# Attention scores on one Trainium2 core: three paired 64-row passes against two stacked 128-row passes a head

## The reference, cut to what matters

```
# first block, "fox": causal attention with a forget term
logits = einsum('bhtd,bhsd->bhts', qb, kb) * d**-0.5 + F[t] - F[s]
probs  = softmax(where(mask, logits, -inf)); o = probs @ v
y_f    = o * silu(fg)

# second block, layer B, "nb": neighbourhood attention on a 64-wide grid plus 256 context tokens
s      = einsum(q_r, k_reg) * scale + bias;  s_ctx = einsum(q_r, kc) * scale
p      = softmax(concat([s, s_ctx]));        o = p_lat @ v + p_ctx @ vc
y      = (o * silu(g)) @ w_out
```

## Time and profile before

| | |
|---|---|
| median of the runs | 3241.89 us |
| span of the profiled execution | 3236.3 us (first to last instruction; the timed runs are 5.6 us longer in the median) |
| PE busy | 3109.7 us, 96% |
| PEld busy | 2578.9 us, 80% |
| DVE busy | 1999.7 us, 62% |
| ACT busy | 1299.9 us, 40% |
| POOL busy | 759.8 us, 23% |
| fox turns | from 603 to 1210 us |
| nb turns | from 2347 to 3110 us |

### The profile page before, as it was taken

How to read it: one execution, slowest core, us unless ns; L and a number is a source line. 1 busy time by engine, 2 the same in 40 slices (tenths; PEclk the granted TensorE clock), 3 DMA queues, 4 the chain that set the end, 5 groups by cost and what they waited for, 6 DMA issues and landing times.

```text
span 3236.3 us, 47842 instructions
## 1 busy us (share of the span) xinstructions
PE 3109.7 (96%) x18134; PEld 2578.9 (80%) x18134; DVE 1999.7 (62%) x3834; ACT 1299.9 (40%) x2340; POOL 759.8 (23%) x324
## 2 busy tenths in 40 slices
PE   9999999999999989999899999999899999999987
PEld 6888888777777767877799889888677778777765
DVE  5676677555565657975755555556755555655555
ACT  5534443444444440022444444440344444454412
POOL 3223332322222213543211121113112112111221
PEclk9999999999999999999999999999999999999999
DMA  3111111111111137521200010153201111100141
GB/s 118 46 40 46 46 59 46 60 59 53 53 53 53 64 146 298 220 79 52 91 30 30 31 43 30 46 203 130 78 21 51 45 51 45 51 32 33 67 161 76
DMA packets 64828, 237.79 MB, mean 73 GB/s; under 512 B 7008, under 2 KB 10080, under 8 KB 63600
## 3 DMA queue, kind: packets, MB, share of 16 engines
q1 hardware_dynamic: 31680, 115.91, 9.9%
q10 hardware_dynamic: 32944, 119.10, 9.7%
HBM read 185.11 MB, written 49.87 MB: 73 GB/s over the span
## 4 chain that ended last, share of the span: by engine, by line
PE 79%; DVE 9%; ACT 5%; issue 2%; DVEq 2%; DMA 1%; ACTq 1%; SPq 0%
PE ps L1304 21%; PE ps L189 13%; PE ps L360 9%; PE ps L2223 7%; PE ps L1368 5%; PE ps L1334 4%; PE ps L1350 4%; PE ps L891 3%; PE ps L482 3%; PE ps L868 2%; PE ps L133 2%; DVE fox_l L1455 1%; PE ps L852 1%; DVE wa_l L941 1%; PE ps L853 1%
## 5 line engine op out<-in xcount | busy, mean ns | idle before, releaser
L210 POOL TENSOR_TENSOR w_hi<-raw,small 128x1024 fp32r<-128x1024 f32 x160 | 334.9, 2093 | 2393.7 <-PE ps L1304 1099.3
L212 POOL TENSOR_TENSOR w_lo<-raw,w_hi 128x1024 fp32r<-128x1024 f32 x160 | 424.8, 2655 | 22.8
L1304 PE MATMUL ps<-nb_u_hi,w_hi 128*128 128x512 f32 (+1 forms) x640 | 249.2, 389 | 6.1 <-DVE nb_q_lo L2470 4.2
L1304 PE MATMUL ps<-nb_u_hi,w_lo 128*128 128x512 f32 (+1 forms) x640 | 246.6, 385 | 0.0
L1304 PE MATMUL ps<-nb_u_lo,w_hi 128*128 128x512 f32 (+1 forms) x640 | 245.7, 384 | 0.0
L1466 DVE TENSOR_TENSOR nb_pt_lo<-ps,nb_pt_hi 128x512 fp32r<-128x512 f32 x208 | 143.9, 692 | 144.2 <-ACT nb_pt_hi L1393 143.9
L360 PE MATMUL ps<-u_hi,w_hi 128*128 128x512 f32 x528 | 212.8, 403 | 5.9 <-ACT silu_h L539 2.6
L1304 PE MATMUL ps<-u_hi,w_lo 128*128 128x512 f32 x512 | 208.9, 408 | 0.0
L360 PE MATMUL ps<-u_hi,w_lo 128*128 128x512 f32 x528 | 208.6, 395 | 0.0
L360 PE MATMUL ps<-u_lo,w_hi 128*128 128x512 f32 x528 | 208.4, 395 | 0.0
L1304 PE MATMUL ps<-u_hi,w_hi 128*128 128x512 f32 x512 | 208.3, 407 | 0.0
(11 more groups left out here) (357 smaller groups left out, 8027.8 us busy)
## 6 DMA issues: line engine op xcount, KB each, us to landing
raw<-in_w_stream SPq DMA_DIRECT2D x160, 512.0 KB, 3.3
h_sb<-in_w_ada ACTq DMA_DIRECT2D x16, 1024.0 KB, 5.0
nf_b<-nf_rows ACTq DMA_DIRECT2D x16, 512.0 KB, 4.4
nb_bias<-in_rel_bias ACTq DMA_DIRECT2D x16, 448.0 KB, 3.8
y_parts<-wa_y_hi ACTq DMA_DIRECT2D x8, 640.0 KB, 3.0
y_parts<-wa_y_lo ACTq DMA_DIRECT2D x8, 640.0 KB, 4.2
la_out_yh<-y_parts SPq DMA_DIRECT2D x8, 640.0 KB, 10.0
la_out_yl<-y_parts SPq DMA_DIRECT2D x8, 640.0 KB, 11.1
```

The costliest lines, as they stand in the source:

```text
L210: pool.tensor_tensor(w_hi[:, s, :], raw[:, s, :], zero, ALU.add)
L212: pool.tensor_tensor(w_lo[:, s, :], raw[:, s, :], w_hi[:, s, :].bitcast(F32), ALU.subtract).then_inc(w_ready, 1)
L1304: mm = pe.matmul(ps[:, b:b + ch["n"]], w(slot, k), u[:, k, ch["c0"]:ch["c0"] + ch["n"]], start=k == 0 and p == 0, stop=k == KT - 1 and p == 2)
```

## The change

Operands: `q_hi`, `q_lo` and the keys get one buffer for each head. `q_hi[hd]` holds the head's high part twice, on both halves of the partitions; `q_lo[hd]` its low part on the head's own half and zeros on the other; `k2[hd]` the keys' high part on the head's half and their low part on the other. Then one 128-row matmul of `q_hi` with `k2` gives q_hi·k_hi + q_hi·k_lo, and one of `q_lo` with `k2` gives q_lo·k_hi: two passes a head where there were three passes for the pair. Evacuations: a Q chunk takes 4 instructions on ScalarE and 2 on VectorE (before 1 and 1), a K chunk 2 and 2 (before 1 and 1), each on 64 partitions. Two memsets of 64x1024 set the zeros, once for fox and once for nb. Signals: `scored` and `shifted` are counted by head, so head 1 of a piece and head 0 are waited for apart. To make room, the gate shares the buffer of the untransposed values (`vt`) instead of its own `silu`, and the window mask of layer A is no longer a part of `consts` but has its own input and its own transfer of 320 KB on ScalarE's queue beside `rope`.

```diff
                     elif step[0] == "S":
                         s = step[1]
-                        pe.wait_ge(self.shifted, s["n"] - 1)
...
-                        for o0, key, n in runs:
-                            for p, (q, k) in enumerate(((self.q_hi, self.k_hi[kv]), (self.q_lo, self.k_hi[kv]),
-                                                        (self.q_hi, self.k_lo[kv]))):
-                                for hd in range(2):
-                                    r = rows_of(hd)
-                                    o = (self.s_bank + hd) * CH + o0
-                                    mm = pe.matmul(ps[:, o:o + n], q[r, qc], k[r, key:key + n],
-                                                   start=p == 0, stop=p == 2)
-                        mm.then_inc(self.scored, 1)
+                        for hd in range(2):
+                            if s["n"] > 1:
+                                pe.wait_ge(self.shifted, self.of_head(s["n"] - 1, hd))
+                            for o0, key, n in s["blk"]["pieces"][s["piece"]]["runs"]:
+                                o = (self.s_bank + hd) * CH + o0
+                                for p, q in enumerate((self.q_hi[hd], self.q_lo[hd])):
+                                    mm = pe.matmul(ps[:, o:o + n], q[:, qc], self.k2[hd][:, key:key + n],
+                                                   start=p == 0, stop=p == 1)
+                            mm.then_inc(self.scored, 1)
...
+            def of_head(self, n, hd):
+                return 2 * n - 1 + hd
...
-                        dve.wait_ge(self.scored, s["n"])
...
                             for hd in range(2):
+                                if i == 0:
+                                    dve.wait_ge(self.scored, self.of_head(s["n"], hd))
...
-                        ins.then_inc(self.shifted, 1)
+                                if i == len(rows[0]) - 1:
+                                    ins.then_inc(self.shifted, 1)
...
+            def queries_high(self, act, ch):
+                src, cols = self.projected(ch), slice(ch["c0"], ch["c0"] + ch["n"])
+                act.wait_ge(self.scored, ch["scored"])
+                for hd in range(2):
+                    for half in range(2):
+                        ins = nc.scalar.activation(self.q_hi[hd][rows_of(half), cols], src[rows_of(hd)], ACT.Copy,
+                                                   scale=HD ** -0.5)
+                ins.then_inc(self.high_out, 1)
+
+            def queries_low(self, dve, ch):
...
+                for hd in range(2):
+                    r = rows_of(hd)
+                    ins = dve.scalar_tensor_tensor(self.q_lo[hd][r, cols], src[r], HD ** -0.5,
+                                                   self.q_hi[hd][r, cols].bitcast(F32), ALU.mult, ALU.subtract)
+                ins.then_inc(self.dve_out, 1)
+
+            def keys_high(self, act, ch):
...
+                for hd in range(2):
+                    ins = nc.scalar.copy(self.k2[hd][rows_of(hd), cols], src[rows_of(hd)])
+                ins.then_inc(self.high_out, 1)
+
+            def keys_low(self, dve, ch):
...
+                for hd in range(2):
+                    r = rows_of(hd)
+                    ins = dve.tensor_tensor(self.k2[hd][rows_of(1 - hd), cols], src[r],
+                                            self.k2[hd][r, cols].bitcast(F32), ALU.subtract)
+                ins.then_inc(self.dve_out, 1)
+
+            def clear_halves(self, dve):
+                for hd in range(2):
+                    dve.memset(self.q_lo[hd][rows_of(1 - hd), :].bitcast(F32), 0.0)
...
-                self.silu = sb(f"{n}_silu", [P, self.q_cols], at=area)
+                self.silu = self.vt[:, self.whole]
...
+            act.dma_start(wa_win[:], a["win"]).then_inc(a_loaded, 16)
...
-            dve.wait_ge(a_loaded, 32)
+            dve.wait_ge(a_loaded, 48)
```

More of the change, by code:

```diff
@@ L1598, in fox_evacuate_dve @@
         def fox_evacuate_dve(dve, ch):
-            src, cols = fox.projected(ch), slice(ch["c0"], ch["c0"] + ch["n"])
             if ch["kind"] == "Q":
-                dve.wait_ge(fox.high_out, ch["out"][1])
-                dve.scalar_tensor_tensor(fox.q_lo[:, cols], src, HD ** -0.5, fox.q_hi[:, cols].bitcast(F32),
-                                         ALU.mult, ALU.subtract).then_inc(fox.dve_out, 1)
+                fox.queries_low(dve, ch)
             elif ch["kind"] == "K":
-                dve.wait_ge(fox.high_out, ch["out"][1])
-                dve.tensor_tensor(fox.k_lo[0][:, cols], src, fox.k_hi[0][:, cols].bitcast(F32),
-                                  ALU.subtract).then_inc(fox.dve_out, 1)
+                fox.keys_low(dve, ch)
         def fox_dve(dve):
```

76 lines of the change are left out of this document (37 added, 39 removed).

## The result

The changed kernel takes 3312.87 us (median of 4 runs, 3308.05 to 3314.34) against 3241.62 us for the kernel before on the same chip (3237.11 to 3244.12). Ratio 1.0218, 95% interval 1.0204 to 1.0233: it is slower by 71 us, where 24 us less were forecast, and the time lies outside the range. The profiled execution has a span of 3306.3 us.

The account below looks back on a forecast made before the run. TensorE, busy 96% of the span, was taken to bound the kernel. Passes -44.7, waits for the other head -12 and evacuations +33 gave -23.7 us on 3236.3, so 3212.6, plus 5.6 for timed runs: 3218 us, range 3190 to 3240.

Parts of the forecast that it names:

- Passes, 44.7 us: Score matmuls on TensorE: two 128-row passes a head avoid the gaps around 64-row pairs, saving 44.7 us.
- Signals by head, 12 us: TensorE's waits ahead of scores: counting by head lets head 0 start earlier, 0.35 us back each time, 12 us.
- Evacuations, 33 us: Extra ScalarE and VectorE copies behind Q and K chunks, and memsets, cost 33 us; bounds 16 and 108.
- Last K chunk: Turn ends: TensorE stands 1.1 us longer 8 times in fox (8.7 us), 0.8 us 7 times in nb (5.6).
- Q chunks and nb's start: First Q chunk of a turn costs 8.8 us in nb, 7.4 in fox; second Q chunk 0; nb's start 2.5.
- Weights are split by GpSimd ... long before they are used: Both Flow phases: GpSimd, busy 18 of 77 us, splits weights early, so it does not bound.
- ScalarE's price, 0.48 us a copy: ScalarE's copies of 64 partitions priced like 128, 0.48 us each; 136 on the path would be 65 us.
- Half price for 64 partitions: Lower bound for the ScalarE and VectorE copies: 64 partitions cost half of 128, 16 us in all.
- The first: Evacuations on ScalarE and VectorE in each turn's group stretch eat the gain: 108 us against 57 won, 3293 us; chance 0.07.
- The second rival: TensorE's gaps belong to the scores' waits and signals, so they stay and passes add 43 us: 3306 us; chance 0.04.
- The third: TensorE's passes shorten but it waits for VectorE and ScalarE; half of 57 us lost, 3242 to 3247; chance 0.10.
- Its mark for "wrong": Prediction fails if passes keep 0.1 us gaps, or TensorE's idle ahead of L1350's and L1368's successors grows much over 20 us.

Follow-up runs that it names:

- e1: Changed kernel with scores taken as three 64-row passes of the two heads side by side, evacuations and per-head signals kept: 3360.86 us, ratio 1.0356.
- e4: Changed kernel with the signals of the two heads joined again, passes and evacuations as changed: 3322.21 us, ratio 1.0230.
- e2: Changed kernel with one 128-partition copy per engine behind each Q or K chunk and no memsets: 3203.98 us, ratio 0.9872.
- e12: Changed kernel with K's copies still split, but Q's copies one 128-partition instruction per engine and no memsets: 3261.76 us, ratio 1.0061.
- e11: Changed kernel with Q's copies still split, but K's copies one 128-partition instruction per engine: 3236.81 us, ratio 0.9984.
- e9: Changed kernel with each head's low copy of Q or K waiting for that head's high copy alone: 3257.43 us, ratio 1.0064.
- e7: Changed kernel with idle matmuls on TensorE at the end of each turn but the last, 12 in fox, 10 in nb: 3306.66 us, ratio 1.0204.

## Why the prediction was wrong

- **Passes, 44.7 us.** Right in kind: all starts are 0.23 us apart, and e1's three paired passes cost 45 us more, in which TensorE's side of the signals is included. They agree with the drain that the Trainium skill states (page "TensorEngine Tiling (Array Packing)", section "Tiling Modes"); that pairs on distinct row groups run at once is outweighed by it, as the prediction said.
- **Signals by head, 12 us.** The listed wait fell to a sixth (a third was forecast), but joining the signals again costs 4 us, which e4's interval tells neither from nothing nor from 12. Passes and signals together gave 41 us in e2, not 57; which of the two terms is too large stays open.
- **Evacuations, 33 us.** This is the step that failed: 112 us by e2. Last K chunk, 8.7 + 5.6 = 14.3 us forecast, 61 to 76 measured (e12 against e2, e11 against the changed kernel), of which 46.5 are listed waits; Q chunks and nb's start, 16.2 + 2.5 = 18.7 forecast, 36 to 51 measured, 30 of them listed waits. With 41 saved and 112 spent the kernel is 71 us slower.
- Where in it. The prediction took a chain that had no slack and added the length of the new instructions, 1.1 us in fox, to it; the wait became 3.3. It left out three things: the low copy waits for both heads' high copies, though only one is its own; the extra copies of the chunk before push y's low part, and so ScalarE's store, ahead of the last high copy; and the SBUF-only instructions of VectorE are pushed across GpSimd's start, where they take 1.8 to 3.5 times as long. For nb it even named the table "between" and gave the place 0.8 us; the wait was 2.5 to 4.6.
- A fourth thing had no term at all: each stall brings the lower clock behind it. Between e2 and the changed kernel that is 34 of the 104 us in the traces. The price of one stretch is seen (1.4 us in a fox turn); what the waits alone would have cost at the full clock was not measured.
- "Weights are split by GpSimd ... long before they are used" was true and beside the point: GpSimd costs nothing by being late, but by when it begins.
- ScalarE's price, 0.48 us a copy, was the pitch of copies of 128 partitions. Those of 64 follow at 0.60 (2.40 for four) and VectorE's at 0.70; ScalarE's busy time grew by 78.7 us for 136 copies, 0.58 each, where 65 us had been the upper bound. Half price for 64 partitions, the lower bound, is out.
- **The rivals.** The first (the evacuations eat it, 3293 us) had the right engines and sign, and 0.07. For its place it named the stretch of transposed groups in each turn, where 27 us of the new waits stand; 46.5 stand at the turn's end. Its own bound, every extra copy on the path, was 108 us; that 112 were measured is luck, since the waits contain y's low part and the tables, and a third of the cost is the clock. The argument against it, that VectorE idles 41 of 95.5 us, was the mistake: idle time of an engine says nothing of the moment at which it is waited for. The second rival fell by e2. The third was half true: of the signals' saving little is shown to have arrived.
- The signs that the prediction named: fox turns 76.2 us forecast, 81.2 measured; nb turns 93.7 and 99.1; the wait for the keys in fox 1.1 and 3.3. Its mark for "wrong", idle time ahead of the transposes and value matmuls up by much more than 20 us, was only just passed: 28.8 us listed before, 54.1 after. Of the 69 us by which idle time grew in all, most stand ahead of the first pieces, where the mark did not look.

## What to carry over

Before a copy is split or an instruction added to an engine with room, look what stands behind it in its queue and when another engine begins: a step that crosses GpSimd's start can cost several times the added time. Price a chain by its waits as well as its lengths, and give each consumer a signal behind the part that it reads; here that gave back 50 of 112 us. Count with a stall the slower matmuls behind it as well. When a saving on the bound engine comes with more work elsewhere, place that work in pieces between the steps that are waited for: the same passes and copies went from 2.2% slower to 0.8% faster by order and signals alone.

## What the runs showed of the hardware

- A VectorE instruction with two SBUF inputs (128x1024) that starts behind GpSimd's split: 2.92 us for 1.22 and 2.21 for 1.23; two of 128x640: 5.35 for 1.55, and 3.26 where the first starts 0.01 us ahead of GpSimd's. One with an input in PSUM: unchanged, 0.69. GpSimd's own went from 1.89 to 2.40 us (675.09 in e9) and 2.57 (2585.20 in the changed kernel) where VectorE's was first.
- Copies of half the partitions cost as much as whole ones and follow less closely: 0.60 and 0.70 us against 0.48 and 0.60. Why the pitch is longer stays open; nothing here tells the shared PSUM bank from the number of partitions.
- After 3.3 us without a matmul the clock is at its lower level for the next 3.15 us; with e7's idle matmuls in that wait it is at the upper one. After 2.48 us without one, at the first Q chunk, it is at the lower level in some turns (824.98) and not in others (743.66, 907.50).
